# A fused two-block transformer kernel: the modulation vector by input tile, the mixer's weights in quarters, its first products one tile ahead

## What is computed

```
h   = rmsnorm(x, norm_mix_g) * (1 + scale_mix) + shift_mix
mix = hybrid_mixer(h, ...)     # h @ w_in, two kinds of causal attention, gates, w_out
x   = x + gate_mix * mix
x   = x + gate_ffn * conv_ffn(rmsnorm(x, norm_ffn_g) * (1 + scale_ffn) + shift_ffn, ...)
```

## Time and profile before

| | |
|---|---|
| median of 3 runs | 1009.71 us (1009.64 to 1009.95) |
| the profiled execution's own time | 1009.63 us |
| its span | 1007.8 us |
| TensorE busy | 998.1 us |
| VectorE, ScalarE busy | 703.2, 590.7 us |
| first product of slice 0 | 18.98 us |

### The profile page before, as it was taken

How to read it: one execution, slowest core, us unless ns; L and a number is a source line. 1 busy time by engine, 2 the same in 40 slices (tenths; PEclk the granted TensorE clock), 3 DMA queues, 4 the chain that set the end, 5 groups by cost and what they waited for, 6 DMA issues and landing times.

```text
span 1007.8 us, 17093 instructions
## 1 busy us (share of the span) xinstructions
PE 998.1 (99%) x6928; PEld 911.5 (90%) x6928; DVE 703.2 (70%) x1179; ACT 590.7 (59%) x987; POOL 0.4 (0%) x5
## 2 busy tenths in 40 slices
PE   9999999999999999999999999999999999999997
PEld 7899999999999999999999888888999899888886
DVE  4698888878888676887658665655766558565652
ACT  4778665557555556767647545554666547455453
POOL 0000000000000000000000000000000000000000
PEclk9999999999999999999999999999999999999999
DMA  9965667535667545453326556455553326555521
GB/s 384 358 245 190 257 233 293 196 148 210 232 256 263 192 162 187 173 209 126 126 88 219 201 203 206 169 183 201 209 189 139 127 105 251 198 178 176 205 80 42
DMA packets 28013, 196.76 MB, mean 195 GB/s; under 512 B 3104, under 2 KB 3744, under 8 KB 4640
## 3 DMA queue, kind: packets, MB, share of 16 engines
q1 hardware_dynamic: 27360, 194.95, 53.3%
q10 hardware_dynamic: 576, 0.72, 0.2%
HBM read 194.61 MB, written 1.05 MB: 194 GB/s over the span
## 4 chain that ended last, share of the span: by engine, by line
PE 96%; ACT 1%; DVE 1%; issue 0%; ACTq 0%; POOLq 0%
PE PS L1011 11%; PE PS L1012 11%; PE PS L1013 11%; PE PS L1195 10%; PE PS L1286 8%; PE PS L1287 8%; PE PS L1288 8%; PE PS L1198 5%; PE PS L1165 3%; PE PS L1168 3%; PE PS L1166 3%; PE PS L1228 2%; PE PS L1230 2%; PE PS L1229 2%; PE PS L1383 2%; PE PS L1372 1%
## 5 line engine op out<-in xcount | busy, mean ns | idle before, releaser
L1830 DVE TENSOR_TENSOR wlo<-raw,whi 128x1024 fp32r<-128x1024 f32 (+1 forms) x314 | 368.2, 1217 | 76.6 <-ACT whi L1448 73.9
L1448 ACT ACTIVATE whi<-raw 128x1024 fp32r<-128x1024 f32 x308 | 306.7, 1047 | 61.8 <-PE PS L1288 55.0
L1011 PE MATMUL PS<-HX,whi 128*128 128x256 f32 x816 | 234.9, 288 | 1.3 <-DVE HX L1804 1.3
L1012 PE MATMUL PS<-HX,whi 128*128 128x256 f32 x816 | 230.8, 283 | 0.0
L1013 PE MATMUL PS<-HX,wlo 128*128 128x256 f32 x816 | 230.7, 283 | 0.0
L1011 PEld LDWEIGHTS PS<-HX,whi 128*128 128x128 f32 x816 | 156.3, 191 | 7.8 <-issue 7.0
L1012 PEld LDWEIGHTS PS<-HX,whi 128*128 128x128 f32 x816 | 156.4, 192 | 0.5
L1013 PEld LDWEIGHTS PS<-HX,wlo 128*128 128x128 f32 x816 | 156.3, 192 | 0.0
L1195 PE MATMUL PS<-HX,whi 128*128 128x512 f32 x416 | 147.9, 398 | 0.0
L1286 PE MATMUL PS<-whi,Oh 128*128 128x512 f32 x344 | 134.6, 391 | 0.0
L1287 PE MATMUL PS<-wlo,Oh 128*128 128x512 f32 x344 | 134.2, 390 | 0.0
(11 more groups left out here) (262 smaller groups left out, 1600.2 us busy)
## 6 DMA issues: line engine op xcount, KB each, us to landing
raw<-wall SPq DMA_DIRECT2D x155, 1024.0 KB, 4.9
raw<-wada SPq DMA_DIRECT2D x18, 1024.0 KB, 5.1
GA<-wada SPq DMA_DIRECT2D x2, 1024.0 KB, 18.2
GA<-alibi SPq DMA_DIRECT2D x1, 2048.0 KB, 9.3
raw<-wall SPq DMA_DIRECT2D x2, 768.0 KB, 5.7
X<-xt SPq DMA_DIRECT2D x1, 1024.0 KB, 5.2
KM<-wada SPq DMA_DIRECT2D x1, 1024.0 KB, 13.2
QF<-wada SPq DMA_DIRECT2D x1, 1024.0 KB, 16.6
```

What stands on the lines that cost most here:

```text
L1011: e.matmul(dst, wh, a, start=start, stop=False, skip_group_check=share)
L1012: e.matmul(dst, wh, b, start=False, stop=False, skip_group_check=share)
L1448: e.activation(whi[place(n)][:, c], raw[i % RAW][:, c], ACT.Copy).then_inc(*up("a_whi", (n, half)))
L1830: e.tensor_tensor(wlo[place(n)][:, c], raw[i % RAW][:, c], f32(whi[place(n)][:, c]), ALU.subtract).then_inc(*up("v_wlo", (n, half)))
```

## The change

- `first_ada[i]` now holds all that one input tile needs: shift and scale of tile i over all eight input tiles, 2 x 128 columns each (`_layout`). So `ada_rows i` is eight matmuls of 256 columns from one 1 MiB load, `ada_columns i` two transposes, and there are eight of each instead of four.
- The bias and the gain of the scale are folded ahead: `silu_c` on VectorE forms `GS = (1 + b_scale) * g` once for all eight tiles; `ada_columns` then does one reduction over two columns, one bias addition for the shift, and `GS += sum * g`.
- The first four chunks are converted in quarters of 512 columns (step `quarter tile piece`), and loaded in halves (one half holds the weights of one input tile). SP's order is tile by tile: the vector's load j, then the half for tile j.
- `mix_tile` writes `Hh` on ScalarE directly from `QM`; VectorE computes `TT` itself (`tensor_scalar`) and then `Hl`. `mix_split` is gone.
- The order in `stages()`: 19 warm-up matmuls instead of 26, then 2 instead of 3, 3, 4 and 7; rows, columns, weights and tile i+1 stand between the parts of tile i; `mix_norm` of tile i+2 behind them; the angle steps in four pieces and the two tables one each behind tiles 4 and 5; `root_table` ahead of `ensure(4)`.
- `positions` and `angles 0` stand before `total`. ACT's queue issues the identity and then the position table only once the small table has landed; the position table lands in `COS` instead of `TT`.
- Loads that reuse the first four buffers wait for the last quarter (mark 3) rather than the last half (mark 1).

```diff
 (stages)
     emit("silu_c")
+    emit("warm", 19, 0)
+    emit("x_squares")
     emit("positions")
-    emit("warm", 26, 0)
-    emit("x_squares")
-    emit("total", "x", 5)
-    emit("ada_rows", 0, 0)
...
+    emit("angles", 0)
+    emit("total", "x", 7)
+    emit("quarter", 0, 0)
+    emit("ada_rows", 0)
+    emit("spread", "x", 7)
+    emit("copy_rms", "x", 7)
+    emit("ada_columns", 0)
+    emit("mix_norm", 0)
+    emit("mix_tile", 0)
+    emit("quarter", 0, 1)
+    emit("mix_norm", 1)
+    emit("warm", 2, 0)
+    for i in range(8):
+        s, parts = i // 2, [(i % 2, t) for t in range(8)]
+        if i == 6:
+            parts = LAST_PARTS[0:6]
+        elif i == 7:
+            emit("slice", s, LAST_PARTS[6:16])
+            break
+        emit("ada_rows", i + 1)
+        emit("slice", s, parts[0:2])
+        emit("ada_columns", i + 1)
+        emit("quarter", i + 1, 0)
+        emit("mix_tile", i + 1)
+        emit("quarter", i + 1, 1)
+        emit("slice", s, parts[2:])
+        if i % 2:
+            st["done"] = s
+        if i < 6:
+            emit("mix_norm", i + 2)
+        if i % 2 == 0:
+            st["have"] = s
+            taken(s)
+        if i in (1, 2, 3):
+            emit("angles", i)
+        elif i in (4, 5):
+            emit("tables", i - 4)
+            if i == 4:
+                emit("final_gain")
+        elif i == 6:
+            emit("signs")
+            emit("root_table")
+            ensure(4)
...
 (SP)
-        for s in range(4):
-            for j in (2 * s, 2 * s + 1):
-                e.dma_start(first_ada[j], wada[j]).then_inc(*up(f"d_ada{j}", 0, 16))
-            load(s)
+        def load_half(s, half):
+            if s in (2, 3):
+                on.wait_ge("t_arow", s - 2)
+            c = slice(half * CH // 2, (half + 1) * CH // 2)
+            e.dma_start(raw[s][:, c], wall[s][:, c]).then_inc(*up(f"d_first{2 * s + half}", 0, 16))
+        for j in range(8):
+            load_ada(j)
+            load_half(j // 2, j % 2)
...
 (TensorE, ada_rows)
+                for k in range(8):
+                    q = k % 4
                     m = e.matmul(
-                        PS[32 * q:32 * q + 32, 4 + p % 2, :],
-                        CA[:, 4 * half + q:4 * half + q + 1].to_broadcast([128, 32]),
-                        first_ada[2 * p + half][:, q * 512:q * 512 + 512], start=half == 0, stop=half == 1)
+                        PS[32 * q:32 * q + 32, 4 + p % 2, 0:256], CA[:, k:k + 1].to_broadcast([128, 32]),
+                        first_ada[p][:, k * 256:k * 256 + 256], start=k < 4, stop=k >= 4)
...
 (ScalarE)
-        e.dma_start(posi, pos).then_inc(*up("d_pos", 0, 16))
-        e.dma_start(ID[:, :], masks[:, 0:128]).then_inc(*up("d_id", 0, 16))
...
+            elif step == "quarter":
+                tile, piece = a
+                n, q = tile // 2, 2 * (tile % 2) + piece
+                on.wait_ge(f"d_first{tile}", 0)
+                if n >= HL:
+                    on.wait_ge("t_mm", chunk_before(n))
+                c = slice(q * CH // 4, (q + 1) * CH // 4)
+                e.activation(whi[place(n)][:, c], raw[n][:, c], ACT.Copy).then_inc(*up("a_whi", (n, q)))
             elif step == "silu_c":
                 on.wait_ge("d_small", 0)
+                e.dma_start(ID[:, :], masks[:, 0:128]).then_inc(*up("d_id", 0, 16))
+                e.dma_start(posi, pos).then_inc(*up("d_pos", 0, 16))
                 e.activation(CA[:, :], col("c", 0, 8), ACT.Silu).then_inc(*up("a_c", 0))
...
-                e.activation(TT[:, i % 2, :], QM[:, i, :], ACT.Identity, scale=GS[:, i:i + 1], bias=ADA[:, i:i + 1]).then_inc(
-                    *up("a_x", i))
+                e.activation(Hh[:, i, :], QM[:, i, :], ACT.Identity, scale=GS[:, i:i + 1], bias=ADA[:, i:i + 1]).then_inc(
+                    *up("a_xhi", ("mix", i)))
...
 (VectorE, ada_columns and mix_tile)
-                for at, c in ((2 * p, 0), (8 + 2 * p, 2)):
-                    m = e.tensor_tensor(
-                        ADA[:, at:at + 2], LM[:, c:c + 2], col("b_ada", at, 2), ALU.add)
...
+                e.tensor_tensor(ADA[:, p:p + 1], LM[:, 0:1], col("b_ada", p), ALU.add).then_inc(*up("v_adab", ("first", p)))
                 e.scalar_tensor_tensor(
-                    GS[:, 2 * p:2 * p + 2], ADA[:, 8 + 2 * p:10 + 2 * p], 1.0, col("norm_mix_g", 2 * p, 2),
-                    ALU.add, ALU.mult).then_inc(*up("v_gs", p))
+                    GS[:, p:p + 1], LM[:, 1:2], col("norm_mix_g", p), GS[:, p:p + 1], ALU.mult, ALU.add).then_inc(
+                    *up("v_gs", p))
...
+                e.tensor_scalar(
+                    TT[:, i % 2, :], QM[:, i, :], GS[:, i:i + 1], ADA[:, i:i + 1], ALU.mult, ALU.add).then_inc(
+                    *up("v_tile", i))
+                on.wait_ge("v_tile", i)
                 low(Hl[:, i, :], TT[:, i % 2, :], Hh[:, i, :], ("mix", i))
...
 (_layout)
-    first = w[:, 0:2048].reshape(2, 4, 128, 2, 4, 256).transpose(4, 0, 2, 1, 3, 5).reshape(8, 128, 2048)
+    first = w[:, 0:2048].reshape(8, 128, 2, 8, 128).transpose(3, 1, 0, 2, 4).reshape(8, 128, 2048)
```

More of the change, by code:

```diff
@@ L290, in stages @@
     emit("silu_c")
+    emit("warm", 19, 0)
+    emit("x_squares")
     emit("positions")
-    emit("warm", 26, 0)
-    emit("x_squares")
-    emit("total", "x", 5)
-    emit("ada_rows", 0, 0)
-    emit("warm", 3, 0)
-    emit("spread", "x", 5)
-    emit("copy_rms", "x", 5)
-    emit("warm", 3, 0)
-    emit("ada_rows", 0, 1)
-    emit("warm", 4, 0)
-    for i in range(4):
-        emit("mix_norm", i)
-    emit("angles", 0)
-    emit("ada_columns", 0)
-    def weigh(s):
-        emit("weights", s, s, (0, 1))
-        st["have"] = s
-        taken(s)
@@ L312, in tile @@
-    def tile(i):
-        emit("mix_tile", i)
-        emit("mix_split", i)
-    emit("weights", 0, 0, (0,))
-    tile(0)
-    tile(1)
-    emit("weights", 0, 0, (1,))
-    st["have"] = 0
-    taken(0)
-    emit("warm", 7, 0)
-    for i in range(4, 8):
-        emit("mix_norm", i)
-    for s in range(3):
-        if s:
-            emit("weights", s + 1, s + 1, (0,))
-        emit("slice", s, PARTS[0:5])
-        emit("ada_rows", s + 1, 0)
-        emit("ada_rows", s + 1, 1)
-        if s == 0:
-            emit("angles", 1)
-            emit("weights", s + 1, s + 1, (0,))
-        emit("slice", s, PARTS[5:8])
-        emit("ada_columns", s + 1)
-        emit("slice", s, PARTS[8:16])
-        st["done"] = s
-        tile(2 * s + 2)
-        emit("weights", s + 1, s + 1, (1,))
-        st["have"] = s + 1
-        taken(s + 1)
-        tile(2 * s + 3)
-        if s == 0:
-            emit("angles", 2)
-            emit("final_gain")
-        elif s == 1:
-            emit("tables")
-        else:
+    emit("angles", 0)
@@ L859, in _build @@
     PBf, PTf = whole(PB), whole(PT)
-    posi = TT[:, 0, :].bitcast(I32)
+    posi = COS[:, :].bitcast(I32)
     ANG = PTf[:, 0:256]
@@ L1455, in scalar @@
                 e.activation(ST[:, 8:9], col("eps"), ACT.Sqrt)
-            elif step == "positions":
-                tt_free[0] = ("v_rope", "positions")
             elif step == "x_squares":
@@ L1832, in vector @@
                         *up("v_wlo", (n, half)))
+            elif step == "quarter":
+                tile, piece = a
+                n, q = tile // 2, 2 * (tile % 2) + piece
+                on.wait_ge("a_whi", (n, q))
+                if n >= HL:
+                    on.wait_ge("t_mm", chunk_before(n))
+                c = slice(q * CH // 4, (q + 1) * CH // 4)
+                e.tensor_tensor(
+                    wlo[place(n)][:, c], raw[n][:, c], f32(whi[place(n)][:, c]), ALU.subtract).then_inc(*up("v_wlo", (n, q)))
+            elif step == "silu_c":
+                on.wait_ge("d_small", 0)
+                e.scalar_tensor_tensor(
+                    GS[:, 0:8], col("b_ada", 8, 8), 1.0, col("norm_mix_g", 0, 8), ALU.add, ALU.mult).then_inc(
+                    *up("v_gs", "base"))
             elif step == "ada_columns":
```

73 lines of the change are left out of this document (37 added, 36 removed).

## The result

The kernel after takes **1012.35 us** (median; 1010.78 to 1013.0), the kernel before 1009.76 on the same chip: 0.22% slower, ratio 1.0022, 95% interval 1.0014 to 1.003. The prediction said 1007.5, with a range of 1006.3 to 1010.2, and gave 0.1 to a time over 1011.7. The runs of one kernel spread more than the few hundredths of a microsecond said at the top: the kernel before took 1009.14 to 1010.30 us in eleven of its twelve runs here, and 1210.74 in one, which does not move the median. The profiled execution after has a span of 1010.3, 2.5 more than the 1007.8 before.

The account below looks back on a forecast made before the run. TensorE bounds the kernel, through how early its real products start and what interrupts them. Earlier start 4.5 + removed wait 0.8 - 1.05 - 0.4 - 0.95 - 0.35 - 0.1 - 0.2 = 2.25; median 1007.5 us, range 1006.3 to 1010.2.

Parts of the forecast that it names:

- It needs about 0.9 us to begin: Prologue: the late-issued identity transfer starts moving about 0.9 us after issue and lands near 7.8 us.
- I take 9.9: Prologue: the position table lands at 9.9 us (bounds 8 and 12.5), so the reciprocal starts at 11.35 instead of 10.3.
- A cast after 11: Sign of being wrong: VectorE casts the position table after 11 us, where about 9.9 was expected.
- B: Rival, prologue: positions land at 12 or after and block VectorE behind the cast; price about 2, 1009.5 us; chance 0.12.
- C: Rival, TensorE's clock: after short idle pieces first products run at the low level; loss 2.7, 1010.2 us; chance 0.1.
- 50.24 - 47.8 - 0.2 = 2.2: Gain: chunk 4 usable at 47.8 instead of 50.24 us, less 0.2 for evacuations after the root table load.
- The rest of the program ... moves with the start: After the prologue: same work in the same order on a bound engine, so it shifts with the start; costed at nothing.
- Rows: Vector's row matmuls: 256-column groups take 0.22 us each, 1.2 per tile; six tiles among the products cost 7.2.
- Rival D: Row matmuls: a group keeps its 0.44 us despite half the columns; 5.2 us more, 1012.7 us; chance 0.06.
- E: Rival, DMA: half loads with 4 KB rows run well below 422 GB/s; 4.4 us at half rate, 1011.9; chance 0.04.
- The wait before tile 7: Tile 6 has 2.40 us of work but tile 7's low part is ready at 3.35: a TensorE stall of 0.95.
- Rival F: Rival: gains are given back by small waits costed at nothing, such as late tiles or evacuations; 1009.5 us; chance 0.13.

Follow-up runs that it names:

- e8: Kernel after, with the identity's transfer issued first of all again and only the position table's behind the small table: 1008.85 us, ratio 0.9996 to the kernel before.
- e2: Kernel after, tables still late, with the position cast and first angle step moved behind tile 1's norm on VectorE: 1009.10 us, ratio 0.9993 to before.
- e3: Kernel after, tables still late, with 12 more warm-up matmuls on TensorE ahead of the spread: 1011.12 us, ratio 1.0013 to the kernel before.
- e4: Kernel after, with 3 warm-up matmuls in TensorE's wait before tile 7 and 1 before chunk 4: 1012.37 us, ratio 1.0024 to before.
- e11: Kernel after, tables late, with the latents' sums woven two at a time behind five groups of chunk 4's products: 1011.61 us, ratio 1.002 to before.
- e9: Kernel after with both tables issued first again and the latents' sums woven two at a time behind five product groups: 1008.86 us, ratio 0.9991 to before.
- e10: Kernel after with both tables issued first again and the latents' ten sums computed twice into the same place: 1013.15 us, ratio 1.0029 to before.
- e6: Kernel after with both tables issued first again and the latents' sums split, kv's behind chunk 4's second half: 1012.59 us, ratio 1.0023 to before.
- e1: Kernel after with the position table and identity issued first on ScalarE's queue again, all else as changed: 1008.28 us, ratio 0.9986 to the kernel before.
- e7: Kernel after with both tables issued first again and four semaphores fewer, first halves using their buffer's own: 1008.60 us, ratio 0.9986 to before.

## Why the prediction was wrong

**The step that failed** is "It needs about 0.9 us to begin", and with it "I take 9.9" for the positions. The 0.9 came from the kernel before, where ScalarE's first issue (0.75) had nothing of SP's ahead but the small table, issued at 0.74. In the kernel after, SP's queue has been given x and 2.5 MiB of weights besides the small table when the identity is issued at 2.99. SP's queue (q1) from 5 to 6 us, then both queues from 6 to 7, 7 to 8 and 8 to 9 (packets, MB, share of 16 engines):

```profile
q1 hardware_dynamic: 66, 0.41, 99.0%
...
q1 hardware_dynamic: 50, 0.41, 97.3%
...
q10 hardware_dynamic: 5, 0.00, 0.8%
...
q1 hardware_dynamic: 49, 0.39, 91.8%
...
q10 hardware_dynamic: 48, 0.02, 8.1%
...
q1 hardware_dynamic: 82, 0.29, 86.8%
...
q10 hardware_dynamic: 82, 0.04, 14.5%
```

ScalarE's queue (q10) moves nothing from 5 to 6 us and 5 packets from 6 to 7, the first at 6.6: it begins 3.6 us after its first issue. Then it goes one for one as forecast, 48 and 49, 82 and 82. The Trainium skill, "DMA: Bandwidth & Descriptors", section "Queues, rings and completion order", says that each engine takes turns between queues by the packet; the trace agrees from 7 us on, but not for the 3.6 us before, in which one queue alone moved packets. The identity landed at 9.8 (forecast 7.8), the positions at 12.7 (forecast 9.9, upper bound 12.5). Most of the 2.8 us is the start: 3.6 us from issue to first packet, where 1.3 was taken. The positions' packets then took 2.9 us behind the identity's, where 2.1 was taken; the three terms that the prediction gives for them add to 2.5, so its own figures say 10.3 and not 9.9. A cast after 11 was one of the prediction's signs of being wrong, and it is at 12.72. What holds the first packet back is not shown. In e8, with the positions issued at 3.21, and in the four other profiles with a late issue (e2, e3, e4, e11), the queue moved nothing before 6.4 us either; in the kernel before, with its first issue at 0.75, it moved 111 packets from 2 to 3 us.

**Two rivals came true together.** B (positions late, price "about 2") measures 2.6 to 2.9, by the estimate under e3. C (the clock, "the loss is the same 2.7") measures 0.8 to 1.1 in the prologue. Together they are the 3.77 us between 47.51 and 51.28. They had chances of 0.12 and 0.10 as if apart; both prices on top of 1007.5 give 1012.2, near the 1012.35 measured, but that is luck: C was priced too high by 1.6 or more, and the second fall and the 0.3 us outside the span fill the place. The prediction's "no stretch of this trace shows it falling" was not quite so either: the kernel before has a clock of 0.50 from 1006.6 to its end at 1007.8, with TensorE's last matmul at 1001.88.

Whether B's wait is what brings the first fall stays open. "TensorE: Matmul & The Clock Gate" of the Trainium skill, Part 1, has the clock halve after idleness; the traces agree with it in part only. For it: in the three kernels in which TensorE idles before the spread (after, e4, e11) the profiled fall lasts 6.8 us, in e9 and e10, without such a wait, 3.4; 32 of their 34 runs have a mean clock of 0.996 or less; and with the wait filled (e3) none of 11 has. Against it as the whole cause: the fall begins 1.7 us before the idle time in e4 and without one in e9 and e10, and e6 idles as long at 1.00. All five profiled falls in the prologue begin within 1.8 us behind the sums of x, 16 one-column matmul instructions in one piece.

**The second fall was nobody's rival.** It comes behind the latents' sums, in 8 of 12 runs of the kernel after by their mean clock. In the profiled one it costs TensorE 1.52 us (2.63 behind the kernel before at the spread, 63.74 against 61.11, and 1.11 behind at the sums of V) and the end 0.8, since VectorE is later than before by 1.68 anyway. The change need not have created it: the kernel before has runs of a low mean clock too (35 of 104), though no profile places their fall. That the latents' sums have a part in it is shown by e11 (in pieces of four instructions: no run of 11 with both falls, against 8 of 12), and e10 (twice as long, a fall of 6.8 us) points the same way. They are not sufficient: e1 runs them in one piece and four of its 11 runs have no fall. The sums of x and of the latents are the only pieces of more than eight one-column instructions in the kernel after, and in all 14 profiles the clock falls behind or within one of these two and nowhere else before TensorE's last matmul. No run took the sums of x apart, so that half of the reading is untested.

**The sum was right for a partly wrong reason.** "50.24 - 47.8 - 0.2 = 2.2" took chunk 4's first product as the point that moves all the rest. In e1 that point moved by 2.73, and the span by 2.1: VectorE's conversion moved from 48.23 to 46.14, by 2.09, and it leads. So e1, which undoes the failed step, still gains 1.5 us in the median and not 2.2: 2.1 in the span, less 0.3 outside it, less falls of the clock in 7 of 11 runs. Before, the product at 50.24 came 0.8 after the half that it needs (48.23 and 1.2); that slack was in the difference and is not to be had. "The rest of the program ... moves with the start" holds for VectorE's start.

**What was right:** 

- Rows: four groups take 0.22 each; a tile 4.27 against 4.32. Rival D (groups keep 0.44) is out, and E too: from 20 to 45 us TensorE is busy 25.00 of 25.00 at 412 GB/s (422 before), so the four added transfers cost it nothing, neither in rate nor as an exposed fixed time.
- Sums of x from 8.26 (8.1), and the first product at 14.5 where the positions are there in time (14.61 in e1, 14.53 in e8).
- The wait before tile 7 is 0.63 idle plus a drained pipeline (0.95 forecast).
- Rival F's "small waits that I cost at nothing": the 0.51 us at 151 is one, from 2.67 to 2.1.

**Not forecast and open:** time less span is 2.16 us after and 1.83 before, 0.3 of the 2.6 us. It stays in e1 and e7, so neither the tables nor four semaphores make it.

The account by profiled runs: VectorE's chain +1.7 (e1's gain of 2.1, less 3.8 for late table and first fall), second fall +0.8, outside the span +0.3: 2.8 for the profiled run, 2.6 in the medians, in which a third of the runs has no second fall.

## What to carry to other kernels

Before moving a small load behind a wait, look at what its queue and the other queue hold at that moment, and at what stands behind its consumer on that engine: here a table that nobody needed early blocked a reciprocal that everybody needed, and moving either the issue (e1) or the cast (e2) gave the gain. When one rival's wait can bring on another rival, here a long idle time and a fall of the clock, give the two together a chance and a price of their own. Before a difference of two profiles is called a price, look whether their inputs were the same: here the table landed 0.69 us apart in the two that were to price the clock. And measure an edit at the engine that leads afterwards: the first product moved by 2.7 us, VectorE's chain and the end by 2.1.

## What the hardware showed unexpectedly

- A transfer of 64 KB on ScalarE's queue took 2.7 us issued first at 0.74 (e8), 5.6 issued behind the positions, and 6.8 issued at 2.99 with another queue's mebibytes ahead, 3.6 of them before its first packet.
- The granted clock fell to 0.50 for 3.4 us with TensorE busy without a break since 51.28, right behind 20 one-column matmul instructions, in two thirds of the runs of one kernel (by mean clock) and in none of another that has them in five pieces. With 40 in a piece it stayed at half for 6.8 us.
- It stayed at 1.00 through 3.12 us without a matmul (e6), and fell 0.7 us into an idle time of 3.15 (after) and 1.7 us before one of 1.82 (e4).
- The same table, issued within 0.1 us in four kernels alike up to there, landed between 12.0 and 12.7 us.
